# Sixteen modulation vectors formed by partition sums on VectorE and GpSimd instead of on TensorE

## The reference

```python
mod_lat = (silu_c @ w_ada[l] + b_ada[l])[:, None, :]
mod_ctx = silu_ctx @ w_ada[l] + b_ada[l]
sh1, sc1, gt1, sh2, sc2, gt2 = jnp.split(mod_lat, 6, axis=-1)
csh1, csc1, cgt1, csh2, csc2, cgt2 = jnp.split(mod_ctx, 6, axis=-1)
h = modulate(rms_norm(x_lat, g_attn[l]), sh1, sc1)     # h * (1 + scale) + shift
x_lat = x_lat + gt1 * gated_merge(...)                 # and gt2 behind the MLP
```

## Time and profile before

| what | value |
|---|---|
| median of three executions | 2072.3 us |
| the profiled execution: span of its instructions | 2069.1 us |
| TensorE busy | 2019.2 us, 98% |
| VectorE busy | 1129.0 us, 55% |
| ScalarE busy | 907.3 us, 44% |
| GpSimd busy | 58.3 us, 3% |
| HBM read | 273.01 MB |

### The profile page before, as it was taken

How to read it: one execution, slowest core, us unless ns; L and a number is a source line. 1 busy time by engine, 2 the same in 40 slices (tenths; PEclk the granted TensorE clock), 3 DMA queues, 4 the chain that set the end, 5 groups by cost and what they waited for, 6 DMA issues and landing times. The chain is left out here.

```text
span 2069.1 us, 31601 instructions
## 1 busy us (share of the span) xinstructions
PE 2019.2 (98%) x12906; PEld 1680.2 (81%) x12906; DVE 1129.0 (55%) x2233; ACT 907.3 (44%) x1632; POOL 58.3 (3%) x83
## 2 busy tenths in 40 slices
PE   5999999999999999999999999999999999999998
PEld 3888767779777777898789899997877678888877
DVE  5447663446433343476665776642465444445886
ACT  4346762335423131265664554443434332233685
POOL 1000000001000000000000000000000000001100
PEclk9999999999999999999999999999999999999999
DMA  8222015533344444443116554444211243222311
GB/s 306 97 92 98 16 49 197 193 132 123 143 183 191 175 163 164 174 172 118 51 63 250 216 187 176 180 167 177 102 45 59 82 173 133 92 96 98 123 62 42
DMA packets 47104, 277.15 MB, mean 134 GB/s; under 512 B 4464, under 2 KB 12784, under 8 KB 16880
## 3 DMA queue, kind: packets, MB, share of 16 engines
q1 hardware_dynamic: 42080, 266.94, 34.2%
q10 hardware_dynamic: 4736, 7.34, 1.0%
q0 software_dynamic: 144, 0.85, 0.1%
HBM read 273.01 MB, written 2.10 MB: 133 GB/s over the span
## 5 line engine op out<-in xcount | busy, mean ns | idle before, releaser
L582 PE MATMUL ps<-t 128*128 128x512 f32 (+1 forms) x2176 | 754.0, 346 | 4.3 <-DVE t L1816 3.3
L584 PE MATMUL ps<-t 128*128 128x512 f32 (+1 forms) x2176 | 747.1, 343 | 0.0
L583 PE MATMUL ps<-t 128*128 128x512 f32 (+1 forms) x2176 | 747.0, 343 | 0.0
L1816 DVE TENSOR_TENSOR t<-t 128x1024 fp32r<-128x1024 f32 (+2 forms) x372 | 416.7, 1161 | 259.5 <-ACT t L1223 258.6
L582 PEld LDWEIGHTS ps<-t 128*128 128x128 f32 x2176 | 410.9, 189 | 68.2 <-issue 8.6
L1223 ACT ACTIVATE t<-t 128x1024 fp32r<-128x1024 f32 (+2 forms) x378 | 359.7, 999 | 222.4 <-PE ps L584 154.1
L584 PEld LDWEIGHTS ps<-t 128*128 128x128 f32 x2176 | 410.9, 189 | 50.6
L583 PEld LDWEIGHTS ps<-t 128*128 128x128 f32 x2176 | 410.9, 189 | 49.8 <-issue 0.7
L1802 DVE TENSOR_TENSOR t<-t 128x512 f32<-128x512 f32 (+10 forms) x621 | 228.8, 389 | 203.4 <-ACT t L1323 73.0
L1323 ACT ACTIVATE t<-ps 128x512 f32<-128x512 f32 (+1 forms) x244 | 115.8, 493 | 345.2 <-PE ps L584 238.6
L1811 DVE SCALAR_TENSOR_TENSOR t<-ps,t 128x256 f32<-128x256 f32 (+2 forms) x176 | 83.1, 496 | 179.8 <-PE ps L584 159.2
(11 more groups left out here) (167 smaller groups left out, 2092.5 us busy)
## 6 DMA issues: line engine op xcount, KB each, us to landing
t<-in_panels SPq DMA_DIRECT2D x235, 1024.0 KB, 4.8
t<-in_panels SPq DMA_DIRECT2D x18, 512.0 KB, 3.6
t<-in_panels SPq DMA_DIRECT2D x8, 768.0 KB, 4.1
t<-in_window ACTq DMA_DIRECT2D x4, 768.0 KB, 4.2
t<-in_ctxT SPq DMA_DIRECT2D x1, 1024.0 KB, 12.1
t<-in_xT SPq DMA_DIRECT2D x1, 1024.0 KB, 14.3
t<-in_ctxT ACTq DMA_DIRECT2D x1, 1024.0 KB, 5.7
t<-in_xT ACTq DMA_DIRECT2D x1, 1024.0 KB, 7.4
```

What stands on the lines that cost most here:

```text
L582: e.matmul(o, hi[:, k, w], xh[:, c0:c1], start=k == 0, stop=False)
L583: e.matmul(o, hi[:, k, w], xl[:, c0:c1], start=False, stop=False)
L584: t = e.matmul(o, lo[:, k, w], xh[:, c0:c1], start=False, stop=k == p.nk - 1)
L1816: e.tensor_tensor(p.half(wlo[p.buf], a), p.half(raw[p.slot], a), p.half(whi[p.buf], a).bitcast(F32), ALU.subtract).then_inc(*up(ve, ("lo", ...
```

## The change

The 64 panels behind the first eight are no longer multiplied on TensorE. Each is summed by partition: for the latent VectorE adds, chunk after chunk, the panel's 128x1024 numbers times the conditioning number of its partition into `parts_of[0]`; for the context GpSimd does the same into `parts_of[1]`, with a product and a sum as two instructions and a buffer `term` between them. When a vector's four panels are in, TensorE adds the 128 partitions with a 128x32 tile `pick` that has ones in one column (`vector_sums`): eight matmuls, or four for the five vectors that only the latent needs (`LATENT_ONLY`; GpSimd leaves these out). The panels now stand one behind each of 64 weight panels instead of two behind each of some thirty, and the vectors come in another order (`VECTORS`) in which those for the latent alone lie between others. A buffer of `raw` that held such a panel is free when VectorE and, for the vectors with a context part, GpSimd have read it. The first panel of a vector (q = 0) may be begun on either engine only when TensorE has done the sums of the vector before.

```diff
+VECTORS = [("b", 0, v) for v in range(6)] + [("b", 1, 2), ("b", 1, 0), ("b", 1, 3), ("b", 1, 1), ("b", 1, 4), ("s", 0, 0), ("s", 0, 1),
+                                             ("b", 1, 5), ("s", 0, 2), ("s", 1, 0), ("s", 1, 1), ("s", 1, 2)]
+LATENT_ONLY = [("b", 1, v) for v in range(2, 6)] + [("s", 1, 2)]
+AFTER = ([(kind, 0, h) for h in range(4) for kind in ("gm", "gn", "no")] + [("wo", 0, a) for a in range(3)] + MLP_PANELS[2:31]
+         + [("gn", 1, h) for h in range(4)] + [(kind, a) for kind in ("mq", "mk") for a in range(4)] + [("mo", a) for a in range(8)])
...
                     if q.whole:
                         e.wait_ge(*done(("used", q.i)))
+                        if q.key[1] >= AT_START and VECTORS[q.key[1] // 4] not in LATENT_ONLY:
+                            e.wait_ge(*done(("used by pool", q.i)))
...
+            def vector_sums(r):
+                key = ("ada", r)
+                o = bank(key, (7,))
+                e.wait_ge(*done(("parts", r)))
+                if VECTORS[r] not in LATENT_ONLY:
+                    e.wait_ge(*done(("context parts", r)))
+                n = 1 if VECTORS[r] in LATENT_ONLY else 2
+                for x in range(n):
+                    for j in range(4):
+                        t = e.matmul(o[32 * j:32 * j + 32, 0:256], pick[:, x, :], parts_of[x][:, j * 256:j * 256 + 256],
+                                     start=x == 0, stop=x == n - 1)
...
             def beside(p):          # VectorE; stands right behind begin(p)
+                if q == 0 and i > AT_START:
+                    e.wait_ge(*done(("full", ("ada", r - 1))))
+                for k in range(2):
+                    c = sc[kind][:, 2 * q + k, 0:1]
+                    if q or k:
+                        own()
+                        stt(parts_of[0][:, :], w[:, k, :], c, parts_of[0][:, :], ALU.mult, ALU.add)
+                    else:
+                        ts(parts_of[0][:, :], w[:, k, :], c, None, ALU.mult, None)
...
+            def beside(key):        # GpSimd
+                for k in range(2):
+                    c = sc[kind][:, 2 * q + k, 1:2]
+                    if q or k:
+                        e.tensor_scalar(term[:, :], w[:, k, :], c, None, ALU.mult).then_inc(*up(po, ("used by pool", a.i)))
+                        e.wait_ge(po.sem, po.n)
+                        e.tensor_tensor(parts_of[1][:, :], parts_of[1][:, :], term[:, :], ALU.add).then_inc(*up(po, ("context parts", r)))
+                        e.wait_ge(po.sem, po.n)
...
-    nc = _bacc.Bacc("TRN2", target_bir_lowering=False, num_devices=1)
+    nc = _bacc.Bacc("TRN2", target_bir_lowering=False, num_devices=1, dynamic_dma_scratch_size=2048)
```

More of the change, by code:

```diff
@@ L141, in plan @@
 def plan():
-    items, late = [], []
+    items = []
     def panel(key, w, k0, nk, n0, n):
         items.append(Panel(key, (*w, k0, n0), nk, n, len(items)))
[L147 to L153, removed]
+        if key in WITH:
+            ada(WITH[key])
     def cols(key, w, k0, nk, n0, n1, first=0):
@@ L340, in program @@
         arow = [sb([128, 256]) for _ in range(2)]
+        parts_of = [sb([128, 1024]) for _ in range(2)]
+        term = sb([128, 1024])
+        pick = sb([128, 2, 32])
         rst = sb([128, T])
@@ L666, in tokens_left, with used @@
                 t.then_inc(*up(pe, ("full", key)))
-            def used(p, first=4):
+            def used(p):
                 mark(pe, ("used", p.i))
-                for i in WITH.get(p.key, [])[:first]:
-                    ada(i)
+                if p.key in WITH:
+                    q = WITH[p.key] % 4
+                    if q == 0:
+                        rows_out()
+                    if q == 3:
+                        vector_sums(WITH[p.key] // 4)
             def xa(k):
@@ L934, in first_layer @@
                     used(p)
[L935 removed]
+                turn(s, at["wo", l, 3], ("wo", l), lambda k: (gYh[:, k, :], gYl[:, k, :]), parts, q0)
                 if last:
                     rms(s, "l")
[L938 to L939 removed]
                     mark(pe, ("xa free", "s0", "c"))
@@ L1841, in beside @@
             def beside(p):
-                for i in WITH.get(p.key, []):
-                    if i % 4 == 0:
-                        rows_out()
-                    taken[0] = i + 1
+                if p.key not in WITH:
+                    return
+                i = WITH[p.key]
+                a, r = at["ada", i], i // 4
+                kind, l, v, q = ADA[i]
+                if q == 1:
+                    rows_out()
+                e.wait_ge(*landed(a))
+                w = a.view(raw[a.slot])
+                if q == 0 and i > AT_START:
[7 more added lines that the diff above has]
+                        ts(parts_of[0][:, :], w[:, k, :], c, None, ALU.mult, None)
+                mark(ve, ("used", a.i), ("parts", r))
+                taken[0] = i + 1
             def fold(kind, l, v, gain):
@@ L2460, in vector @@
             e.memset(power[:, :], -0.5).then_inc(*up(ve))
+            e.memset(pick[:, :, :], 0.0).then_inc(*up(ve))
+            own()
+            for x in range(2):
+                e.memset(pick[:, x, x:x + 1], 1.0).then_inc(*up(ve))
             e.memset(epst[:, :], EPS).then_inc(*up(ve, "ones"))
@@ L2498, in norm_mod @@
                             *up(po, ("xlo", s, k, x)))
+            def beside(key):
+                i = WITH[key]
+                a, r = at["ada", i], i // 4
+                kind, l, v, q = ADA[i]
+                if VECTORS[r] in LATENT_ONLY:
+                    return
+                e.wait_ge(*landed(a))
+                w = a.view(raw[a.slot])
+                if i == AT_START:
+                    for n in "bs":
+                        e.wait_ge(*done(("sc", n)))
+                elif q == 0:
+                    e.wait_ge(*done(("full", ("ada", r - 1))))
+                for k in range(2):
[5 more added lines that the diff above has]
+                        e.wait_ge(po.sem, po.n)
+                    else:
+                        e.tensor_scalar(parts_of[1][:, :], w[:, k, :], c, None, ALU.mult).then_inc(*up(po, ("context parts", r)))
+                        e.wait_ge(po.sem, po.n)
             for l in range(2):
-                q0 = CTX if l else 0
                 norm_mod(f"n1.{l}", "cl")
                 lo(at["uq", l, 0])
+                for h in range(4):
+                    for kind in ("gn",) if l else ("gm", "gn", "no"):
+                        beside((kind, l, h))
+                if not l:
+                    for a in range(3):
+                        beside(("wo", 0, a))
                 norm_mod(f"n2.{l}", "l" if l else "cl")
+                if not l:
+                    for key in MLP_PANELS[2:31]:
+                        beside(key)
             e.wait_ge(*done(("ff2 end", 1, 3)))
@@ L2508, in gpsimd @@
             norm_mod("s0", "l")
+            for kind in ("mq", "mk"):
+                for a in range(4):
+                    beside((kind, a))
             for i in range(16):
@@ L2511, in gpsimd @@
                 rsqrt(ssc, ssc, ("h mean", i), ("h root", i))
+            for a in range(8):
+                beside(("mo", a))
             lo(at["atkv", 0])
```

29 lines of the change are left out of this document (14 added, 15 removed).

## The result

The changed kernel takes 2149.7 us in the median of four executions (2146.2 to 2156.7), the kernel before 2071.8: ratio 1.038 (95% interval 1.036 to 1.040), 78 us slower where 10 were forecast. The sign is right, the size is not, and the time lies far above the range.

The account below looks back on a forecast made before the run. TensorE was taken as the bound, busy 2019.2 of 2069.1 us. From 2072.3 us, 40 less for TensorE's own balance and 50 more for waits gave 2082 us, range 2047 to 2106.

Parts of the forecast that it names:

- What bounds the kernel: Whole kernel: TensorE is the bound, busy 2019.2 of 2069.1 us; VectorE and GpSimd have room on average.
- What leaves TensorE: Vector panels on TensorE: 54 of 64 count, at 1.03 us each, so 55 us leave.
- What VectorE gets: Sixteen vectors' additions on VectorE: product 0.75 us, product-and-sum 1.27 us, 154 us more in all.
- What GpSimd gets: Eleven context vectors on GpSimd: product 1.3 us, sum 2.4 us, 27 us a vector, 300 us in all.
- The loop that decides: Three panel buffers: landing, split and additions take 10.9 us per weight panel, against TensorE's 11.3.
- What lengthens the ring: GpSimd and VectorE block one another in SBUF: 3.3 us more a context panel (q = 0 to 2), making 14.2.
- the ring: Round of the three panel buffers: a weight panel loads only after the vector panel three places ahead is read; 10.9 us.
- Price by place: TensorE waits at context vectors: MLP 28 us, mLSTM 14, layer 0's gates 8, others 1 to 2; about 50 us.
- The first: The forecast itself: the ring with collisions exceeds TensorE's pace and waits eat more than the gain; 2082 us, chance 0.5.
- The second: GpSimd-VectorE collisions cost less than half of the count, below some 1.5 us a panel: 2037 to 2060 us, chance 0.33.
- The third: GpSimd's product is as slow as its sum, 2.4 us, so VectorE waits 4.4 us a panel: 2106 us, chance 0.1.

Follow-up runs that it names:

- order alone: New order of panels and vectors, but TensorE multiplies all 64 panels as in the kernel before; VectorE and GpSimd add nothing: 2116.6 us, ratio 1.022.
- private tiles: Changed kernel with GpSimd doing as many operations on two tiles of its own, nobody waiting for it, context's result left out: 2145.5 us, ratio 1.036.

## Why the prediction was wrong

**What bounds the kernel.** Right: TensorE. In the new order its relief is worth 65 us (order alone against no GpSimd part) with three buffers and 51 with four.

**"What leaves TensorE"** is the step that failed first. It took 54 panels at 1.03 us off and let the order cost nothing. Lone panels cost 1.20, so more could be saved, but the comparison with the kernel before has to pay for the order: 46 us, 26 of them for want of a buffer (shown by the fourth), 11 for lone panels (argued from the timeline), the other 9 open. In the changed kernel not all of this applies, as there TensorE doesn't multiply them; what is left of it is seen in the run without GpSimd's part: 19 us faster than before, where the prediction's -40 belongs. With a fourth buffer it is 31 us, so 12 of the missing 21 are again the buffer. By stage, the run without GpSimd's part gains 1.6 us in layer 0's gates and output projection, 16.3 in the MLP and 7.8 in mLSTM, and loses 5.9 in layer 1 ahead of its MLP. (One reading is off without effect: the three panels end at 874.57 us, not 874.67.)

**"What VectorE gets"** was right in the pure prices: 1.28 and 0.78 us against 1.27 and 0.75. **"What GpSimd gets"** was wrong: its product takes 2.84 us at the least and 3.47 on average, and neither 1.3 nor the upper bound of 2.4 held. One operand is not cheaper there than two. A page of the Trainium skill ("GPSIMD Engine Reference", section "4.1 Engine selection") that puts one-operand work near line rate led the same way; the measurement decides against it for this operation. Waiting for GpSimd's results and reads is worth only 4 us (private tiles against the changed kernel). But a longer product can also block VectorE for longer, and no run separates how much of the 94 us comes from that.

**"The loop that decides"** and **"What lengthens the ring"** were right as a mechanism, and close in the MLP: 10.9 predicted (its terms add up to 10.8) and 11.0 measured without GpSimd, 14.2 predicted and 14.0, 13.2 and 12.6 measured with it. That the latter is so near is partly luck: the 3.3 us of collisions stood on a product of 1.3 us, which takes over twice that, and VectorE is held up 2.7 us a panel. VectorE's product-and-sum has a mean of 1.54 us, not 1.9. The fourth buffer takes 64 of the longer chain's 92 us away where VectorE adds both parts, which shows the ring for that kernel; for the changed one it is carried over from the equal cost.

**"Price by place"** is the other step that failed: about 50 us given back were forecast and 98.6 measured, 28 against 36 in the MLP, 14 against 26 in mLSTM, 8 against 37 in layer 0's gates. In the MLP the price of a vector was right, 7 us, but not the count: sums of five context vectors stand in that stage (at 561.32, 660.37, 759.63, 858.06 and 909.87 us) and four were priced. In mLSTM, 568.7 against 542.9 us, two were priced and a third follows at `mo`. The three vectors at layer 0's gates are the large miss. The kernel with GpSimd's part takes 515.0 us to the end of this stage, the one without 478.4. The prediction took the panels there to be longer. Half of them are of 512 KB and take TensorE half as long, two of each head pair, so TensorE's pace per vector panel is not slower than in the MLP but about the same. This removes the reason for a low price; why a vector costs 12 us there and 7 in the MLP stays open. Late landing alone isn't it: the 1 MB panels issued from 303 to 465 us take 6.5 us in the median with GpSimd's part and 6.2 without.

The clock was no term of the sum at all. Of the 98 us between the two spans with and without GpSimd's part, 73 are idle time of TensorE and 25 are busy time, most of it matmuls at the lower clock behind the waits (1.93 instead of 1.07 us for a group of sums). Whether they are a loss of their own beside the ring, the run with eight added matmuls answers only in part.

**Sum by these runs:** before 2071; new order 46 more; TensorE's relief 65 less; the longer chain 94 more; waiting for GpSimd 4 more: 2150. The forecast's 40 less stands against 19 less here, its 50 more against 98 more: 21 and 48 us, which make up the 68 by which the forecast was short.

**Rivals.** The first was the case, with twice the cost that it gave the waits. The second, that collisions are short, is refuted by the run with private tiles, where VectorE loses 2.7 us a panel (it needed less than 1.5). The third's condition, a product on GpSimd as slow as its sum, was fulfilled and exceeded; its price of 4.4 us a panel was not (the ring grew by 1.6 to 3.0).

## What to carry to other kernels

Before work is taken off the bound engine, write down for how long each transfer buffer is held, and by whom: with three buffers and two kinds of panel in turn, a reader that needs 2.5 us more per panel lost 92 us on an engine that was 64% busy, and with a fourth buffer it lost 28. Price a new order by itself, as a kernel that changes nothing else; here it hid a loss of 46 us behind a gain of 65. Count the places one by one: eleven context vectors stood in the order, and the forecast priced nine. And a sum over engines that finish late should be asked for a step later than it is complete: the versions that did this, in the old order and without GpSimd, gained 1% (what the later sums alone are worth was not run).

## What the runs showed of the hardware

- GpSimd's product of 128x1024 float32 numbers with one scalar a partition took at least 2.84 us, its sum of two tensors of that size 2.34.
- VectorE's product with a scalar was blocked by GpSimd too: 0.78 us alone, 1.52 on average beside it, 2.88 at the place shown.
- Matmuls of 32x256 float32 results cost 0.12 us each when four in a row stand on four column tiles and 0.44 when all stand on one.
- Between two tile shapes TensorE lost about 0.34 us for the change and the way back: a lone group cost 1.20 us and a pair 2.06, so a group by itself is 0.86 and the rest is paid once for each visit.
- Lifting the granted clock from 0.971 to 0.980 of its full value gave no time back in this kernel.
